# Keeping five weight units of one expert in idle buffers, a resequenced wide pass, and the general branch moved to the end of TensorE's program

## What is computed

```python
logits = xf @ w_router + b_router
top_v, top_i = lax.top_k(logits, TOP_K)               # 4 of 32 experts for each token
gates = softmax(top_v)
def expert_block(xb, e):                              # xb: the tokens sent to expert e
    g = xb @ w_gate[e] + b_gate[e]                    # 1024 x 1024
    u = xb @ w_up[e] + b_up[e]                        # 1024 x 1024
    g = jnp.minimum(g, 7.0)
    u = jnp.clip(u, -7.0, 7.0)
    glu = g * jax.nn.sigmoid(1.702 * g)
    return ((u + 1.0) * glu) @ w_down[e] + b_down[e]  # 1024 x 1024
out = sum over the chosen experts of gate * expert_block
```

## Time and profile before

| | us |
|---|---|
| median of 3 runs (lowest, highest) | 2140.27 (2140.13, 2140.76) |
| the profiled execution's own time | 2141.08 |
| its span, first to last instruction | 2139.3 |
| TensorE matmuls busy | 2073.1 (97%) |
| VectorE, ScalarE busy | 569.8 (27%), 403.1 (19%) |
| data moved | 562.26 MB, mean 263 GB/s |
| granted TensorE clock, mean | 0.993 of full |

### The profile page before, as it was taken

The page is one execution under the profiler, slowest core; times in us unless marked ns, Lnnn a source line. Parts: engine busy times, 40 slices in busy tenths (PEclk is TensorE's granted clock), DMA queues, the critical chain, the costliest instruction groups (busy, mean ns, idle before and its releaser), DMA issues. The chain is left out here.

```text
span 2139.3 us, 26280 instructions
## 1 busy us (share of the span) xinstructions
PE 2073.1 (97%) x9730; PEld 1307.6 (61%) x9731; DVE 569.8 (27%) x1251; ACT 403.1 (19%) x776; POOL 6.1 (0%) x23
## 2 busy tenths in 40 slices
PE   8999899999999999999999999999999999999999
PEld 7677333333343344333333676888888886888888
DVE  4633111111111121111111457221000794220001
ACT  3431122111211221221111122220000222310000
POOL 0000000000000000000000000000000000000000
PEclk9998899999999999999999999999999999999999
DMA  8254799999989998999999833424344433334420
GB/s 323 79 192 180 282 412 422 422 422 422 422 338 410 422 371 338 423 422 422 422 422 422 358 116 118 177 99 154 143 155 157 160 126 128 118 113 146 155 79 20
DMA packets 78302, 562.26 MB, mean 263 GB/s; under 512 B 8832, under 2 KB 9216, under 8 KB 10144
## 3 DMA queue, kind: packets, MB, share of 16 engines
q1 hardware_dynamic: 77328, 554.94, 65.3%
q0 software_dynamic: 912, 6.42, 0.7%
HBM read 557.14 MB, written 4.19 MB: 262 GB/s over the span
## 5 line engine op out<-in xcount | busy, mean ns | idle before, releaser
L424 PE MATMUL bank<-xn,ring 128*128 128x256 f32 x2144 | 470.2, 380 | 0.9 <-ACT B L1199 0.6
L798 PE MATMUL bank<-ring,B 128*64 128x512 f32 x1920 | 431.1, 599 | 24.7 <-DMA ring<-in_stream 18.0
L424 PEld LDWEIGHTS bank<-xn,ring 128*128 128x128 f32 x2144 | 407.6, 190 | 61.9 <-issue 5.6
L1199 ACT ACTIVATE B<-bank 128x512 f32<-128x512 f32 (+3 forms) x294 | 152.6, 530 | 1205.0 <-PE bank L424 425.8
L798 PEld LDWEIGHTS bank<-ring,B 128*64 128x64 f32 x1920 | 131.7, 137 | 302.1 <-issue 238.3
L817 PE MATMUL bank<-ring,B 128*64 128x512 f32 x960 | 212.6, 595 | 0.0
L1116 PE MATMUL bank<-B,ring 128*128 128x256 f32 x704 | 155.2, 379 | 0.0
L1116 PEld LDWEIGHTS bank<-B,ring 128*128 128x128 f32 x704 | 133.8, 190 | 18.2
L817 PEld LDWEIGHTS bank<-ring,B 128*64 128x64 f32 x960 | 66.3, 137 | 125.0 <-issue 125.0
L1961 DVE TENSOR_TENSOR B<-bank,mbias 128x512 f32<-128x512 f32 x34 | 23.5, 691 | 412.2 <-PE bank L783 412.2
L424 PE MATMUL bank<-xg,ring 128*128 128x256 f32 x416 | 99.3, 393 | 10.8 <-DMA ring<-in_stream 9.4
(11 more groups left out here) (309 smaller groups left out, 1486.1 us busy)
## 6 DMA issues: line engine op xcount, KB each, us to landing
ring<-in_stream SPq DMA_DIRECT2D x524, 1024.0 KB, 14.6
mem_kv<-ring POOLq DMA_DIRECT2D x2, 1024.0 KB, 7.0
B<-mem_kv POOLq DMA_DIRECT2D x2, 1024.0 KB, 6.2
xT<-in_x SPq DMA_DIRECT2D x1, 1024.0 KB, 4.9
ring<-in_mem SPq DMA_DIRECT2D x1, 1024.0 KB, 17.8
mem_kv<-xg POOLq DMA_DIRECT2D x1, 1024.0 KB, 4.1
xg<-mem_kv POOLq DMA_DIRECT2D x1, 1024.0 KB, 5.4
out_y<-xT SPq DMA_DIRECT2D x4, 256.0 KB, 2.3
```

The source lines that it names most:

```text
L424: mm = pe.matmul(dst[:, m, :], tile(u, m * C + k), rhs[:, k, :], start=(k == 0), stop=(k == C - 1))
L798: mm = pe.matmul(PS[4 + kind][NARROW * h:NARROW * (h + 1), :], xs[:, k % 4, NARROW * (k // 4):NARROW * (k // 4 + 1)], ring[:, expert_slot( ...
L1199: return act.activation(out_, in_, fn, **kw)
```

## The change

Three parts. Where the text says expert 24, KEPT = 24.

1. Units 7 to 11 of expert 24 are loaded before the experts into `xg`, `xn`, `sq`, `prob` with `pT`, and `tsq` with `tv`, with ten DMAs of 0.5 MB. Their turns in the ring are kept by small DMAs of 16 x 16 floats (`mark_slot`), so that all counts stay as they were. TensorE takes the common expert loop apart: a loop over experts 0 to 23, a copy of the body for expert 24 that reads the kept buffers, and a loop over 25 to 31. SP's loop is taken apart in the same way.
2. On TensorE the general branch moves behind the whole program; the common branch follows the test directly.
3. The wide pass goes unit by unit: each gate and up unit is used for both halves of the hidden width and freed at once. Gate and up halves have a bank each (4, 5 and 6, 7), the transposes go into banks 4 and 5 in turn, `select_T` goes between units 9 and 10 of down, and the next expert's `turn_tokens` goes behind down. ACT and DVE follow (`wide_halves`; `swiglu` returns `gate` and `product`).

```diff
+KEPT = 3 * E // 4
+KEPT_UNITS = (7, 8, 9, 10, 11)
-        ge = reg(5120, 512)
-        ue = reg(5632, 512)
+        ge = [reg(5120, 512), gA[1]]
+        ue = [reg(5632, 512), uA[1]]
+        kept = {8: (flat(xn)[:, 0:D], flat(xn)[:, D:2 * D]), 9: (flat(sq)[:, 0:D], flat(sq)[:, D:2 * D]),
+                7: (flat(xg)[:, 0:D], flat(xg)[:, D:2 * D]), 10: (flat4(prob), flat4(pT)),
+                11: (flat(tsq), flat(tv))}
@@ SP
-            with sp.Fori(1, turns) as i:
+            def keep(j):
+                u = AT["moe"] + 12 * KEPT + j
+                for kk in range(2):
+                    sp.dma_start(kept[j][kk], stream[u][:, D * kk:D * (kk + 1)]).then_inc(S["kept_loaded"], 16)
+            def mark_slot(i, s):
+                sp.wait_ge(S["units_done"], i * RING + (EARLY + s - RING + 1))
+                sp.dma_start(ring[0:16, s, 0:16], stream[i * RING + (EARLY + s)][0:16, 0:16])\
+                    .then_inc(landed[s], 16)
+            sp.wait_ge(S["o_mm"], 8)
+            sp.wait_ge(S["ksum_mm"], 4)
+            keep(10)
+            keep(11)
+            for s in range(RING):
+                if s == MOE_AT:
+                    keep(8)
+                    sp.wait_ge(S["stat_mm"], STATS[1] + 1)
+                    keep(9)
+                    sp.wait_ge(S["tok_mm"], 4)
+                    keep(7)
+                load_slot(1, s)
+            with sp.Fori(2, KEPT) as i:
                 for s in range(RING):
+                    load_slot(i, s)
+            for i in (KEPT, KEPT + 1):
+                for s in range(RING):
+                    (mark_slot if RING * i + s - MOE_AT - 12 * KEPT in KEPT_UNITS else load_slot)(i, s)
+            with sp.Fori(KEPT + 2, turns) as i:
+                for s in range(RING):
+                    load_slot(i, s)
@@ TensorE, wide_pass after turn_tokens(n, 1)
+                for j in range(6):
+                    await_expert_unit(e, j)
+                    for kk in range(2):
+                        for w in range(2):
+                            mm = gate_up(j, kk, w)
+                            if frees and j and kk == w == 0:
+                                mm.then_inc(S["units_done"], 1)
+                turn_wide(n, 0, 0)
+                turn_wide(n, 1, 0)
                 for w in range(2):
...
+                    for j in (6, 7):
+                        if w == 0:
+                            await_expert_unit(e, j)
+                        for kk in range(2):
+                            mm = gate_up(j, kk, w)
...
+                turn_wide(n, 0, 1)
                 pick_tokens(n + 1, 0)
-                turn_tokens(n + 1, 0)
-                pe.wait_ge(M["h_ready"], nth(n, 1))
-                select_T(n, False)
-                pe.wait_ge(M["selT_ready"], n + 2)
+                turn_wide(n, 1, 1)
+                pe.wait_ge(M["h_ready"], nth(n, 0))
                 for j in range(8, 12):
                     await_expert_unit(e, j)
+                    if j == 10:
+                        pe.wait_ge(M["h_ready"], nth(n, 1))
+                        select_T(n, False, PS[4])
...
+                turn_tokens(n + 1, 0)
+                pe.wait_ge(M["selT_ready"], n + 2)
                 pe.wait_ge(M["y_ready"], n + 2)
@@ TensorE, the experts
+            def experts(one):
+                with pe.Fori(0, KEPT) as e:
+                    one(e)
+                pe.wait_ge(S["kept_loaded"], 160)
+                one(KEPT)
+                with pe.Fori(KEPT + 1, E) as e:
+                    one(e)
-            with pe.If(most > WIDE):
...
-            with pe.Else():
...
+            pe.br_cond(most > WIDE, "pe_general", "pe_common")
+            pe.bass.switch_bb("pe_common", parent=entry)
+            first_tokens()
+            experts(expert)
...
+            pe.br("pe_rest")
+            pe.bass.switch_bb("pe_rest", parent=entry)
@@ TensorE, behind the last feed-forward layer
+            pe.br("pe_done")
+            pe.bass.switch_bb("pe_general", parent=entry)
+            first_tokens()
+            experts(expert_in_blocks)
...
+            pe.br("pe_rest")
```

More of the change, by code:

```diff
@@ L774, in await_expert_unit, with weights, turn_wide @@
                 pe.wait_ge(landed[expert_slot(j)], e * 16 + 16 * expert_loads(j))
+            def weights(e, j, kk, h):
+                if isinstance(e, int) and j in kept:
+                    return kept[j][kk][:, 512 * h:512 * (h + 1)]
+                return ring[:, expert_slot(j), D * kk + 512 * h:D * kk + 512 * (h + 1)]
+            def turn_wide(n, w, kind):
+                pe.wait_ge(M[("g_ready", "u_ready")[kind]], nth(n, w))
+                if kind:
+                    pe.wait_ge(M["sig_in"], nth(n, 1))
+                    if w:
+                        pe.wait_ge(M["xgt_ready"], nth(n + 1, 0))
+                for c in range(4):
+                    mm = pe.transpose(PS[4 + (w ^ kind)][:, c * P:(c + 1) * P],
+                                      (gA, uA)[kind][w][:, c * P:(c + 1) * P], tb("ident"))
+                mm.then_inc(M[("tg_mm", "tu_mm")[kind]], 1)
             def turn(n, w, kind):
@@ L837, in wide_pass, with gate_up @@
                 mm = None
-                for w in range(2):
[L839 to L856, removed]
+                def gate_up(j, kk, w):
+                    kind, k = j // 4, 2 * (j % 4) + kk
+                    mm = pe.matmul(PS[4 + 2 * kind + w][:, :], xw[:, k, :],
+                                   weights(e, j, kk, w),
+                                   start=(k == 0), stop=(k == C - 1))
+                    if k == C - 1:
+                        mm.then_inc(M[("g_mm", "u_mm")[kind]], 1)
+                    return mm
@@ L883, in tokens_of, with expert, expert_in_blocks @@
                 return pe.value_load(load[0:1, bass.ds(e, 1)], min_val=0, max_val=T)
+            def expert(e):
+                pe.wait_ge(M["xs_ready"], nth(e, 0))
+                with pe.If(tokens_of(e) < NARROW + 1):
+                    narrow_pass(e, e)
+                with pe.Else():
+                    wide_pass(e, e, True)
+                pe.nop()
+            def expert_in_blocks(e):
+                for b in range(BLOCKS):
+                    pe.wait_ge(M["xs_ready"], nth(e * BLOCKS + b, 0))
+                    wide_pass(e * BLOCKS + b, e, b == BLOCKS - 1)
@@ L897, in _ @@
-            with pe.Else():
[L898 to L909, removed]
+            entry = pe.bass.cur_bb
@@ L1977, in dve_pass @@
                 select(n + 1, ne, nb, general, step)
-                swiglu(n, e, 0, wide, step)
+                gate, product = swiglu(n, e, 0, wide, step)
+                gate()
                 if wide:
-                    swiglu(n, e, 1, wide, step2)
+                    gate2, product2 = swiglu(n, e, 1, wide, step2)
+                    gate2()
+                    product()
+                    product2()
                     assert step2.n == STEPS2
+                else:
+                    product()
                 dve.wait_ge(M["selT_mm"], n + 1)
```

111 lines of the change are left out of this document (67 added, 44 removed).

## The result

| | before | after |
|---|---|---|
| median of 4 runs, us | 2140.36 | 2119.19 |
| lowest to highest | 2140.13 to 2140.76 | 2118.47 to 2119.65 |
| ratio, 95% interval | | 0.9901 [0.9883, 0.9918] |
| span of the profiled execution | 2139.3 | 2117.3 |

The forecast was 2119.9 us. The sum came out, but by luck: its terms missed in both directions, and that is what the experiments are about.

The account below looks back on a forecast made before the run. DMAs were taken to bound experts 0 to 11 and the end of 19 to 31, TensorE the rest. Terms -9.4 - 2.8 - 8.2 = -20.4 us took 2140.27 to 2119.9 us, range 2115 to 2130.

Parts of the forecast that it names:

- DMAs set the ends of the first and the third stretch: Experts 0 to 11 end by DMA at 568.17 us; experts 19 to 31 hold 16.55 us of DMA waits.
- First term: Start through expert 11: earlier expert 0 and a warm (short) first jump give -9.4 us, bounds 0 and -11.7.
- 128 x 2.485 = 318.1, so 543.5 us, against 552.88: Expert 1 to expert 11's last gate-up unit: DMAs bring 128 units from 225.4 us, ending at 543.5.
- the queue is free at 213 + 12.4 = 225.4 us: Before expert 1: five kept units add 12.4 us, delaying its loads by no more than about 1.5 us.
- I cost the price at nothing: At the start: kept loads fill the DMAs' idle stretch and cost nothing; without that stretch 12.4 us.
- The bound of -11.7: Start through expert 11: the first term's largest gain, TensorE's bound when no DMA wait is added.
- Second term: Wide passes of experts 12 and 18: less TensorE idle, -1.4 us each, -2.8 in all, bounds -5 and +3.
- Third term: Experts 19 to 31: five units fewer to load but one cold jump, 363.2 us against 371.45, so -8.2.
- I take one cold of two: Jumps over the wide pass at expert 24 and the loop behind: one stalls long, costing 7.3 us.
- the rival with no cold jump: Experts 19 to 31: neither new jump stalls, 359.0 us, -12.4; in all -24.6, 2115.7 us; chance 0.12.
- The rival that the marks cost as much as full DMAs: Experts 19 to 31: marks cost 2.3 us each, stretch gains about -0.9; in all -13.1, 2127.2 us; chance 0.03.
- the slower one: From expert 24 on: the jump over the wide pass stalls each pass, up to +36.9 us, 2177.1; chance 0.05.

Follow-up runs that it names:

- x1: The changed kernel with part 2 undone, so the general branch stands ahead of the common one on TensorE again: 2123.35 us.
- x4: The changed kernel without kept units and marks, with one loop over the experts on TensorE and SP (parts 2 and 3 alone): 2127.01 us.
- x6: The changed kernel with keep(10) and keep(11) issued ahead of SP's wait for the spilled keys: 2114.15 us.
- x9: The changed kernel with 24 recorded semaphore increments on TensorE ahead of its test of the counts, shifting all later code: 2120.15 us.
- x10: As x6, but the kept buffers serve two experts: units 7 to 11 of expert 6, then of expert 24, loaded at SP's turn 14: 2102.52 us.
- x3: The changed kernel with the five marks as full 1 MB ring loads again, kept buffers still read: 2131.53 us.
- x7: The changed kernel with all five kept loads moved from the start to SP's turn 14, between the two wide passes: 2113.70 us.

## Why the prediction came out

- *DMAs set the ends of the first and the third stretch, and what TensorE gains in the first is lost to them.* Right: expert 0 came 6.4 us earlier and its jump was warm, 14.7 us in all by expert 2 (269.12 against 283.84), and expert 12 came 6.6 us earlier. In x1, x4, x6 and x9 too expert 12's start follows what the DMAs have to bring, not TensorE's own sum; in x10, where the DMA waits are gone, it follows TensorE's.
- *First term, -9.4; measured -6.6.* The step that failed is "128 x 2.485 = 318.1, so 543.5 us, against 552.88". The step before it, "the queue is free at 213 + 12.4 = 225.4 us", was nearly right. The view of the DMAs from 190 to 226 us has

```profile
DMA packets 2630, 13.76 MB, mean 382 GB/s; under 512 B 306, under 2 KB 306, under 8 KB 1598
```

  and the eight ring loads and five kept units are 13 x 1.0486 = 13.63 MB, a load of 0.13 MB beside them: expert 1's loads began at about 226.0. With 318.1 us for the 128 units the last data is there at 544.1, but the last gate-up unit of expert 11 starts on TensorE at 546.28. I had set the end of a transfer against the start of a matmul, and left out what lies between them, some 2.2 us of the 2.8 by this sum; the other 0.6 is the queue. What the 2.2 us consist of no run separates. A store of 256 KB takes 2.6 us from issue to landing here. "I cost the price at nothing" failed too: x4 shows 5.2 us for the kept units. The term of -9.4 had this price in it without saying so, since it began expert 1's loads at 225.4 us and not at 217, when they can be issued with expert 0 at 214. The conditions of keep(10) and keep(11) were met at 163 us, but I did not say what SP was queued behind: its wait for the spilled keys, to 190 us. x6 moves them and gets 5.3 us back. The bound of -11.7 was wrong too: TensorE alone, 215.2 + 12 x 27.30 = 542.8, would allow -25.4; x4 has -11.8 and x10 -23.6.
- *Second term, -2.8; measured -4.4.* Right in kind. The idle fell from 3.8 to 2.35 us a pass, 1.4 each as I took, if not in the places where I had put it. The view by line of expert 18's pass:

```profile
L907 PE MATMUL bank<-ring,B 128*128 128x512 f32 x64 | 27.9, 594 | 0.8 <-ACT B L1299 0.8
...
L954 PE MATMUL bank<-B 128*128 128x256 f32 x16 | 3.7, 384 | 0.8 <-ACT B L1299 0.8
L838 PE MATMUL bank<-tab,B 128*128 128x128 f32 x16 | 2.3, 276 | 0.7 <-ACT B L1299 0.7
```

  The 0.8 of xs_ready and the 0.7 of the picked tokens stayed, y_ready's 1.2 fell to 0.8, h_ready never waits. The other 0.8 us a pass lies in busy time, 55.05 us before and 54.26 after for expert 18. Groups that follow each other without a stop overlap, and there are fewer stops: the transposes took 2.5 us in the earlier trace rows and take 2.3 here (L838). I had counted the matmuls as equal, and they are, but not their edges; how the 0.8 us divides among them is not shown.
- *Third term, -8.2; measured -11.4.* "I take one cold of two" failed: the changed kernel's branch at expert 24 is 2.3 us long and shows as 0.40 us of idle, and expert 25's is warm. What came is nearest to the rival with no cold jump, which had -12.4 for this term and 0.12 as its chance. x1 has the cold one at expert 24 (363.6 us, where I had 363.2), x9 the one at expert 25 (361.2). I had 7.3 us for a cold jump: x1 shows 4.12 of idle and 2.65 through the clock, 6.8 in all, and x9 at expert 25 4.46 and 1.70, 6.2. So its size was about right; which of them are cold was chance of placement, and x9 shows that 24 instructions decide it. And the price of one is smaller than I took where DMA waits follow.
- *The rule of the Trainium skill* ("Runtime: NRT & Kernel Launch", section "Instruction fetch mechanics"), by which code comes in blocks in sequence and a taken branch out of them stalls, agrees with x9, x1 and the changed kernel: long branches occur once for each place and not in later passes of a loop, and an unedited jump changes with the length of the code in front. x3's longer branch with the same code is not explained by it.
- *The sum* was right to 0.7 us by luck: the first term's error of +2.8 was met by -1.6 and -3.2 of the others, and the medians moved 0.8 us less than the spans.

The rival that the marks cost as much as full DMAs is refuted by x3 against the changed kernel, the slower one by the branches of L966: none is long in experts 26 to 31.

## What to carry to other kernels

In a kernel whose stretches alternate between two bounds, price a saving by what comes behind it in its own stretch: five units less to load brought 12.3 us where DMA waits followed, and nothing directly ahead of a pass that had none. A transfer ahead of its need is free where its queue rests (x6) or where the loads behind it have a lead to spare (x7), and only if its issue is not held by an earlier wait; look at what the issuing engine is queued behind, not at when the condition is met. A copied loop body is to be priced as one stall of some 6 to 8 us (idle and the lower clock behind it) at each jump to code that was not run yet, or a part of that, or none, depending on where the code falls; DMA waits behind it take that stall back.

## What the runs showed of the hardware

- The records of the experts' branch on TensorE were 0.17 us long at the median, and 5.9 to 6.9 us at some of the jumps to code that had not been run; 24 instructions in front decided at which (x9). In between lie 1.1 us (x1, expert 0), 2.3 us (the changed kernel, expert 24) and, with the same code on TensorE, 3.7 us (x3).
- The sequencer runs ahead of the matmuls, so a branch shows only in part: 6.2 us as 4.7 us of idle (x9, expert 0) and 2.3 us as 0.4.
- Behind an idle of 4 to 5 us the granted clock fell from 2.4 to 1.2 GHz (0.50 in 982 to 986 us of x1): the narrow pass behind x1's cold jump takes 29.9 us in place of 27.3. In x3 an idle of 1.79 us was enough (0.50 in 978 to 980 us; gate and up take 15.65 us in place of 13.95). In the changed kernel, with 0.40 us there, the clock stays at 1.00 from 213 us to the end of the experts.
- DMAs of 1 KB in a full queue of 1 MB loads took 12.1 us (median) to landing and cost the stream nothing that can be seen.
